# A mixture-of-experts encoder: one half of the activations turned in blocks by VectorE and carried by ScalarE, and the norm weight applied by ScalarE instead of GpSimd

## What is computed

```python
u = rmsnorm(h, norm_ffn_g)                      # row / rms(row) * g, g of 1024 weights
aff = softmax(u @ router_w)                     # per token, over 16 experts
gate, idx = top_k(aff.T, 64)                    # each expert picks 64 of the 512 tokens
xs = u[idx]                                     # 64 rows x 1024; 128 rows for both trunks
hid = silu(xs @ w_gate[e]) * (xs @ w_up[e])     # 128 x 2048
out = (hid @ w_down[e]) * gate
h[idx] += out
```

## Time and profile before

| | |
|---|---|
| median of 3 runs | 1543.75 us |
| the profiled execution's own time | 1543.18 us |
| its span, first to last instruction | 1541.4 us |
| TensorE matmul, busy | 1529.7 us, 99% |
| VectorE, busy | 1309.9 us, 85% |
| ScalarE, busy | 1043.1 us, 68% |
| GpSimd, busy | 225.9 us, 15% |

### The profile page before, as it was taken

The page is one execution under the profiler, slowest core; times in us unless marked ns, Lnnn a source line. Parts: engine busy times, 40 slices in busy tenths (PEclk is TensorE's granted clock), DMA queues, the critical chain, the costliest instruction groups (busy, mean ns, idle before and its releaser), DMA issues.

```text
span 1541.4 us, 22566 instructions
## 1 busy us (share of the span) xinstructions
PE 1529.7 (99%) x8318; PEld 1236.9 (80%) x8318; DVE 1309.9 (85%) x1386; ACT 1043.1 (68%) x985; POOL 225.9 (15%) x140
## 2 busy tenths in 40 slices
PE   9999999999999999999999999999999999999997
PEld 7888878888863888888888888888888888888886
DVE  7684886684865999999999999999999999998987
ACT  6454655353452777777777777777778777777777
POOL 0000010000022222120221303022120312210012
PEclk9999999999999999999999999999999999999999
DMA  9543447333476999999999999999999999999998
GB/s 344 188 144 118 148 146 278 96 124 123 149 255 232 409 419 404 387 414 372 405 389 395 400 377 414 361 421 392 379 405 385 406 382 403 389 385 409 365 395 330
DMA packets 156407, 498.60 MB, mean 323 GB/s; under 512 B 10880, under 2 KB 36608, under 8 KB 156352
## 3 DMA queue, kind: packets, MB, share of 16 engines
q1 hardware_dynamic: 144624, 461.54, 77.1%
q0 software_dynamic: 9280, 31.07, 6.5%
q10 hardware_dynamic: 2448, 5.25, 1.3%
HBM read 473.70 MB, written 20.97 MB: 321 GB/s over the span
## 4 chain that ended last, share of the span: by engine, by line
PE 96%; DMA 1%; DVE 1%; ACT 1%; issue 0%; SPq 0%; POOLq 0%; POOL 0%; DVEq 0%; ACTq 0%
PE ps L1977 81%; PE ps L2025 4%; PE ps L2032 2%; PE ps L2136 2%; PE ps L2076 1%; PE ps L2445 1%; PE ps L2294 1%; PE ps L2082 1%; DMA u_rows<-arena 1%; DMA raw<-w_qkv 0%; PE ps L2582 0%; PE ps L2290 0%; PE ps L2312 0%; DVE arena L1388 0%; SPq L591 0%
## 5 line engine op out<-in xcount | busy, mean ns | idle before, releaser
L1314 DVE TENSOR_TENSOR w_rest<-raw,w_high 128x2048 fp32r<-128x2048 f32 x212 | 506.9, 2402 | 65.8 <-ACT w_high L1191 48.0
L1191 ACT CAST w_high<-raw 128x2048 fp32r<-128x2048 f32 x184 | 352.5, 1916 | 139.5 <-PE ps L1977 139.5
L1977 PE MATMUL ps<-w_high,xt_high 128*128 128x512 f32 x984 | 304.5, 389 | 0.0
L1977 PE MATMUL ps<-w_rest,xt_high 128*128 128x512 f32 x984 | 304.3, 389 | 0.0
L1977 PE MATMUL ps<-w_high,xt_rest 128*128 128x512 f32 x984 | 304.3, 389 | 0.0
L1977 PEld LDWEIGHTS ps<-w_high,xt_high 128*128 128x128 f32 x984 | 184.6, 188 | 39.2 <-issue 0.8
L1314 DVE TENSOR_TENSOR w_rest<-early,w_high 128x2048 fp32r<-128x2048 f32 x90 | 206.7, 2299 | 10.8 <-ACT w_high L1191 10.7
L1977 PEld LDWEIGHTS ps<-w_high,xt_rest 128*128 128x128 f32 x984 | 184.7, 188 | 38.4
L1977 PEld LDWEIGHTS ps<-w_rest,xt_high 128*128 128x128 f32 x984 | 184.7, 188 | 38.2
L1314 DVE TENSOR_TENSOR w_rest<-raw_more,w_high 128x2048 fp32r<-128x2048 f32 x92 | 206.6, 2284 | 6.1 <-ACT w_high L1191 6.1
L1191 ACT CAST w_high<-early 128x2048 fp32r<-128x2048 f32 x90 | 172.3, 1916 | 58.1 <-PE ps L1977 58.1
(11 more groups left out here) (310 smaller groups left out, 2205.5 us busy)
## 6 DMA issues: line engine op xcount, KB each, us to landing
raw<-w_down SPq DMA_DIRECT2D x64, 1024.0 KB, 7.8
raw<-w_gate SPq DMA_DIRECT2D x62, 1024.0 KB, 8.1
raw<-w_up SPq DMA_DIRECT2D x62, 1024.0 KB, 8.0
raw_more<-w_down SPq DMA_DIRECT2D x32, 1024.0 KB, 8.2
early<-w_down SPq DMA_DIRECT2D x32, 1024.0 KB, 8.7
raw_more<-w_gate SPq DMA_DIRECT2D x31, 1024.0 KB, 8.2
raw_more<-w_up SPq DMA_DIRECT2D x31, 1024.0 KB, 8.4
early<-w_gate SPq DMA_DIRECT2D x31, 1024.0 KB, 8.6
```

What stands on the lines that cost most here:

```text
L1191: nc.scalar.copy(w_high[:, i % SLOTS, :], src).then_inc(high_done, 1)
L1314: nc.vector.tensor_tensor(w_rest[:, j, :], src, w_high[:, j, :].bitcast(F32), ALU.subtract).then_inc(rest_done, 1)
L1977: done = nc.tensor.matmul(out, lhs, rhs, start=start and part == 0, stop=stop and part == 2)
```

## The change

Four things change. The first half of the activations (`acts[0]`) is no longer turned by TensorE within the loop: VectorE transposes the 32 x 32 blocks within each group of 32 partitions (`turn_blocks`), ScalarE copies each of the 16 combinations of a group of token rows and a group of feature columns to its group of partitions (`moves`, 32 rows x 256 floats each), casts the outcome (`moved_high`), and VectorE subtracts (`moved_rest`). GpSimd's product with the norm weight is gone; ScalarE applies it on the turned rows, where a feature is a partition, in 8 activations of 128 x 128 with a scale per partition (`weigh_rows`), which write into another tile. The four loads of the spread norm weight become one small load of a column form. Two semaphores are merged at the start of expert 0.

```diff
 def next_rows(e):                       # GpSimd
     gather(e + 1)
-    pool.wait_ge(gathered, 16 + 16 * QUARTERS * (e + 1))
-    tokens = xg.rearrange("p (t n) -> p t n", t=QUARTERS)
-    weights = piece_g.rearrange("p (t n) -> p t n", t=1).broadcast_to([P, QUARTERS, SPAN])
-    nc.gpsimd.tensor_tensor(tokens, tokens, weights, ALU.mult).then_inc(rows_scaled, 1)
...
-    for a in range(QUARTERS):
-        on, of = slice(a * QUARTER, (a + 1) * QUARTER), slice(a * SPAN, (a + 1) * SPAN)
-        pool.dma_start(piece_g[on, :], g_ffn[:, of].broadcast_to([QUARTER, SPAN])).then_inc(grow_in, 16)
+    pool.wait_ge(nmx_done, HEADS * TRUNKS)
+    pool.dma_start(piece_g, g_ffn_pieces).then_inc(grow_in, 16)
...
+def weigh_rows(e):                      # ScalarE
+    if isinstance(e, int) and e == 1:
+        act.wait_ge(grow_in, 16 * 2)
+    act.wait_ge(rows_turned, e)
+    act.wait_ge(xtr_done, e + 1)
+    for k in range(KC):
+        at = slice(k * P, (k + 1) * P)
+        nc.scalar.activation(weighted_rows[:, at], turned_rows[:, at], ACT.Copy, scale=piece_g[:, k:k + 1]).then_inc(rows_scaled, 1)
...
+def moves(f, lo, hi):                   # ScalarE
+    if lo == 0:
+        act.wait_ge(turn_step, TURN_STEPS * f + 1)
+        act.wait_ge(htr_done, 2 * f + 1)
+    for n in range(lo, hi):
+        a, c = n % QUARTERS, n // QUARTERS
+        tokens, columns = slice(a * QUARTER, (a + 1) * QUARTER), slice(c * QUARTER, (c + 1) * QUARTER)
+        nc.scalar.copy(to_chunks[columns, :, tokens], from_blocks[tokens, :, columns]).then_inc(turn_step, 1)
+
+def moved_high(f):
+    act.wait_ge(turn_step, TURN_STEPS * (f + 1))
+    act.wait_ge(pair_used, pairs_before(f) + 28)
+    nc.scalar.copy(ht[0][0][:, :], shuffled).then_inc(hth_done, 1)
...
 act.wait_ge(gate_done, TRUNKS)          # ScalarE, expert 0
+weigh_rows(1)
 rows_high(1)
...
-highs(0, 30, 33)
+highs(0, 30, 31)
+weigh_rows(2)
+highs(0, 31, 33)
 rows_high(2)
...
 with act.Fori(1, E - 2) as f:
     highs(f, 12, 19)
     step_silu(2 * f + 2, pairs_before(f) + 16, 0)
-    highs(f, 19, 28)
+    highs(f, 19, 24)
+    for i in range(24, 28):
+        highs(f, i, i + 1)
+        moves(f, 2 * (i - 24), 2 * (i - 23))
     step_silu(2 * f + 3, pairs_before(f) + 25, 1)
-    highs(f, 28, 31)
+    for i in range(28, 31):
+        highs(f, i, i + 1)
+        moves(f, 2 * (i - 24), 2 * (i - 23))
+        if i == 28:
+            weigh_rows(f + 2)
     rows_high(f + 2)
-    highs(f, 31, 32)
-    hidden_high(2 * f + 2, 0, 2)
-    highs(f, 32, 36)
-    hidden_high(2 * f + 3, 1, 6, pairs_before(f) + 32)
+    highs(f, 31, 33)
+    moves(f, 14, 16)
+    highs(f, 33, 34)
+    moved_high(f)
+    highs(f, 34, 36)
+    hidden_high(f + 4, 1, 6, pairs_before(f) + 32)
     result(f, pairs_before(f) + 32)
...
+def turn_blocks(f):                     # VectorE
+    dve.wait_ge(turn_step, TURN_STEPS * f)
+    dve.wait_ge(hid_done, 2 * f + 3)
+    nc.vector.transpose(blocks, acts[0]).then_inc(turn_step, 1)
...
 turn_rows(f + 2)                        # VectorE, in the loop
-rests(f, 19, 28)
+rests(f, 19, 21)
+turn_blocks(f)
+rests(f, 21, 28)
 step_hidden(2 * f + 3, 1)
 rests(f, 28, 31)
 rows_rest(f + 2)
-rests(f, 31, 32)
-hidden_rest(2 * f + 2, 0, 2)
-rests(f, 32, 36)
+rests(f, 31, 34)
+moved_rest(f)
+rests(f, 34, 36)
 hidden_rest(2 * f + 3, 1)
...
 def all_turns(e):                       # TensorE; e is a register in the loop
     pe.wait_ge(hid_done, 2 * e + 2)
     pe.wait_ge(htr_done, 2 * e)
     if not isinstance(e, int):
         pe.nop(nofuse=True)
-    hidden_t(acts[0], 2)
+    if isinstance(e, int):
+        hidden_t(acts[0], 2)
     hidden_t(acts[1], 6)
```

More of the change, by code:

```diff
@@ L139 @@
 QUARTERS = P // QUARTER
+MOVES = QUARTERS * QUARTERS
+TURN_STEPS = 1 + MOVES
 SPAN = D // QUARTERS
@@ L163, with encoder_kernel @@
 ROW_BANKS = (4, 6)
-def encoder_kernel(nc, x, x_t, g_mix, g_ffn_col, g_ffn, g_fin, w_qkv, bias, w_o, router_w, w_gate, w_up, w_down, identity, y):
+def encoder_kernel(nc, x, x_t, g_mix, g_ffn_col, g_ffn_pieces, g_ffn, g_fin, w_qkv, bias, w_o, router_w, w_gate, w_up, w_down, identity, y):
     h_dram = nc.dram_tensor("h_rows", [TRUNKS * T, D], F32).ap()
@@ L293, in encoder_kernel @@
         spread_rows = lg
-        piece_g = grow[:, 0:SPAN]
+        piece_g = mx[:, :, :].rearrange("p a i -> p (a i)")
+        weighted_rows = h_more[:, 0, :]
         quadrant = var[:, 27:28]
@@ L302, in encoder_kernel @@
         acts = (silu, hid)
+        blocks, shuffled = arena[:, 0, :], arena[:, 1, :]
+        from_blocks = blocks.rearrange("p (m n) -> p m n", n=P)
+        to_chunks = shuffled.rearrange("p (m n) -> p m n", n=P)
         ht = ((ht_high, ht_rest), (odd_high, odd_rest))
@@ L361, in encoder_kernel @@
         scaled = sem("scaled")
+        turn_step = sem("turn_step")
         rows_scaled = sem("rows_scaled")
@@ L406, in encoder_kernel @@
         third_silu_done, third_hid_done = sem("third_silu_done"), sem("third_hid_done")
-        half_silu = sem("half_silu")
         first_xt_done = sem("first_xt_done")
@@ L739, in _ @@
                     nc.gpsimd.tensor_tensor(early_rows, early_rows, grow[0:CAP, :], ALU.mult).then_inc(early_scaled, 1)
-                    pool.wait_ge(early_scaled, 1)
-                    for a in range(QUARTERS):
-                        on, of = slice(a * QUARTER, (a + 1) * QUARTER), slice(a * SPAN, (a + 1) * SPAN)
-                        pool.dma_start(piece_g[on, :], g_ffn[:, of].broadcast_to([QUARTER, SPAN])).then_inc(grow_in, 16)
+                    pool.wait_ge(nmx_done, HEADS * TRUNKS)
+                    pool.dma_start(piece_g, g_ffn_pieces).then_inc(grow_in, 16)
                 for k in full:
@@ L801, in scatter @@
                                         compute_op=ALU.add).then_inc(scattered, 16)
-            pool.wait_ge(grow_in, 16 * (1 + QUARTERS))
             next_rows(0)
@@ L810, in _ @@
             scatter(E - 2)
-            pool.wait_ge(rows_scaled, E - 1)
+            pool.wait_ge(early_scaled, 1)
+            pool.wait_ge(grow_in, 16 * 2)
             load_grow(g_fin)
@@ L815, in _ @@
             pool.indirect_dma_start(last_h, None, h_dram, last_rows).then_inc(last_in, 16)
-            pool.wait_ge(grow_in, 16 * (2 + QUARTERS))
+            pool.wait_ge(grow_in, 16 * 3)
             for t in SCALED_TILES:
@@ L1158, in rows_high, with hidden_high @@
                     return
-                act.wait_ge(rows_turned, e)
-                nc.scalar.copy(xt_high[:, :], turned_rows).then_inc(xth_done, 1)
-            def hidden_high(s, odd, banks=6, used_by_down=None):
-                act.wait_ge(ht_mm, s + 1)
+                act.wait_ge(rows_scaled, KC * e)
+                nc.scalar.copy(xt_high[:, :], weighted_rows).then_inc(xth_done, 1)
+            def weigh_rows(e):
+                if isinstance(e, int) and e == 1:
+                    act.wait_ge(grow_in, 16 * 2)
+                act.wait_ge(rows_turned, e)
+                act.wait_ge(xtr_done, e + 1)
+                for k in range(KC):
+                    at = slice(k * P, (k + 1) * P)
+                    nc.scalar.activation(weighted_rows[:, at], turned_rows[:, at], ACT.Copy, scale=piece_g[:, k:k + 1]).then_inc(rows_scaled, 1)
+            def hidden_high(turns, odd, banks=6, used_by_down=None):
+                act.wait_ge(ht_mm, turns)
                 if used_by_down is not None:
@@ L1215, in _ @@
             act.wait_ge(first_half, 1)
-            nc.scalar.activation(silu[CAP:P, 0:BANK], ps[0:CAP, 0:BANK], ACT.Silu).then_inc(half_silu, 1)
+            nc.scalar.activation(silu[CAP:P, 0:BANK], ps[0:CAP, 0:BANK], ACT.Silu).then_inc(early_silu, 1)
             step_silu(0, GU_PAIRS - 1)
-            hidden_high(0, 0, 0)
+            hidden_high(1, 0, 0)
             highs(0, 8, 11)
@@ L1222, in _ @@
             act.wait_ge(gate_done, TRUNKS)
+            weigh_rows(1)
             rows_high(1)
             highs(0, 11, 14)
-            hidden_high(1, 1)
+            hidden_high(2, 1)
             highs(0, 14, 21)
@@ L1229, in _ @@
             step_silu(3, pairs_before(0) + 27, 1)
-            highs(0, 30, 33)
+            highs(0, 30, 31)
+            weigh_rows(2)
+            highs(0, 31, 33)
             rows_high(2)
             highs(0, 33, 34)
-            hidden_high(2, 0, 2)
+            hidden_high(3, 0, 2)
             highs(0, 34, 36)
-            hidden_high(3, 1, 6, pairs_before(0) + 32)
+            act.sem_inc(turn_step, TURN_STEPS)
+            hidden_high(4, 1, 6, pairs_before(0) + 32)
             result(0, pairs_before(0) + 32)
@@ L1251, in _ @@
             highs(E - 2, 20, 24)
-            hidden_high(2 * E - 2, 0)
+            hidden_high(E + 2, 0)
             highs(E - 1, 0, D_PAIRS)
@@ L1268, in _ @@
             h_square(0)
-            act.wait_ge(ht_mm, 2 * E)
+            act.wait_ge(ht_mm, E + 3)
             nc.scalar.copy(xt_high[:, 0:BANK], bank(6)).then_inc(hth_done, 1)
@@ L1808, in rows_rest @@
                 dve.wait_ge(xth_done, e + 2)
```

(19 more changed lines are left out.)

## The result

The changed kernel takes 1546.37 us, the median of 15 runs (1545.82 to 1548.23), against 1543.63 us (1542.45 to 1544.32, 15 runs) before: a ratio of 1.002, 95% interval 1.0013 to 1.0028. So it is a little slower, by 2.7 us. That is 0.18%, just inside the 0.2% that I had called no change, though the interval reaches past it. The forecast was 1543.8 and its own range 1540.7 to 1547. The profiled execution spans 1544.8 us; before it was 1541.4.

A forecast was written before the change was run, and what follows sets the result against it. TensorE alone was taken to bound the kernel; per turn, 0.49 us saved less waits of 0.23 and 0.26 left 0.0. Profiled 1543.2 plus 0.57 gave 1543.8 us; own range 1540.7 to 1547, with rivals 1537.2 to 1550.

The forecast's parts named there:

- What is saved: TensorE loses 16 of 32 transposes in 13 turns: 0.49 us per turn, 6.4 us in all, the most possible gain.
- The move: ScalarE's copy of 32 x 256 floats: 0.40 us long, costing 0.42 to the next start.
- The hold: On ScalarE, a changed partition group removes the 0.10 us overlap: cast and two moves take 2.78 us, otherwise 2.42.
- The weighing: ScalarE's 128 x 128 activation with a scale per partition: 0.29 us each, eight in 2.33, behind pair 28's cast.
- The Silu: In ScalarE's queue between pairs 27 and 28: 0.92 us to the next start.
- The chain to pair 31: ScalarE's queue from pair 24's cast at 945.10 to pair 31's cast at 968.63, which started at 964.10 before.
- rival B: ScalarE's small or held instructions before pair 31 cost 0.02 to 0.03 us more each: 6.5 us, 1550; chance 0.27.
- The waits: TensorE waits twice per turn: 0.23 us at pair 31 for its subtraction, 0.26 at pair 33 for `moved_rest`.
- The hand-over of 0.15: TensorE resumes 0.05 us after VectorE's subtraction ends, and its first matmul takes 0.33 instead of 0.23: 0.15 in all.
- The total: Per turn, gain 0.49 us and waits 0.49: nothing left, 0.0 us; 1543.8 us, chance 0.42 for within 0.2%.
- A, no hold: ScalarE's moves overlap like other instructions, TensorE never waits, all 6.4 us stay: 1537.4; chance 0.13.
- C, memory: Transfers are the next limit, so the change doesn't matter: 1543.8 as well, within the 0.42 for no change.

The follow-up runs named there:

- early_weigh: Changed kernel with all 8 weighings of a turn behind pair 21's cast instead of pair 28's, moves unchanged: 1536.31 us.
- one_group: Changed kernel with all 16 moves copying within the first group of 32 partitions, into four tiles, turned half not put together: 1536.02 us.
- silu_order: Changed kernel with moves 4 to 7 in the order 5, 6, 7, 4, so the last before the Silu reads the first group: 1544.52 us.
- one_early: Changed kernel with one of the 8 weighings behind pair 21's cast, the other 7 still behind pair 28's: 1542.51 us.

## Why the prediction came out as it did

- **What is saved.** Predicted 0.49 us per turn; early_weigh, which has nothing left but this, has turns of 66.15 against 66.66: 0.51, and 7.0 us in all where I had 6.4. Right, a little small.
- **The move**, predicted 0.40 long and 0.42 apart: 403 ns and 0.43. **The hold**: right, and decisive, as one_group shows. A cast and two moves took 2.79 us on the mean rather than 2.78, 0.08 us in six; pair 24's and the cast of the rows took 0.01 more each.
- **The weighing**: 0.389 long, eight in 2.36 us instead of 2.33.
- **The Silu.** This is the largest term that was wrong, half of what the chain missed: "Silu 0.92: 957.02". It cost 1.05, because the cast behind it is held by the move ahead of it. I had applied the hold to neighbours only. The page of the Trainium skill cited ahead (VectorE: DVE Perf Modes, Two Vector instructions with no wait between them) words the rule by memory, comparing with the last instruction that read or wrote that memory; read so, it gives the Silu's case, and the traces of ScalarE agree in all five places looked at (1.05, 0.93, 0.93, 1.03, 0.92 us). It is worth 1.7 us (silu_order).
- **The chain to pair 31**: predicted 968.63 - 945.10 = 23.53 us, measured 970.63 - 946.84 = 23.79. The 0.26 missed are the 0.08 and 0.02, the 0.03 and the 0.13 above. I had also counted twelve moves ahead of pair 31's cast where the order has 14, two behind each of pairs 24 to 30; the sum had them all, the count of 18 instructions for its steepness and for rival B did not.
- **The waits**: predicted 0.23 and 0.26 at pairs 31 and 33, measured 0.41 and 0.34, at just those places and for those reasons. The first is not 0.26 longer, as the chain is, since TensorE came to pair 31 later by itself: its three pairs behind the transposes took 8.29 us (966.33 to 974.17 + 0.455) and not 3 x 2.73 = 8.19, because 2.73 is a mean and the first two matmuls behind the transposes are slower too. That this error of 0.10 worked against the other was luck. The hand-over of 0.15 was 0.05 (974.87 to 974.92) and 0.11 at the first wait; at the second it was 0.13 (`moved_rest` ends at 979.38 + 1.22) and 0.10, and this is all that the second wait has over its 0.26.
- **The total**: waits of 0.75 less 0.51 saved make 0.24 of the 0.28 us by which the turns grew; where the other 0.04 lies I don't know. 13 x 0.28 are 3.6 us instead of 0; the profiled spans differ by 3.4, the medians by 2.7. The "nothing is left" was the difference of two terms of 0.49 us, and it was off by more than half of one of them: the balance was right, its zero was not.
- **Expert 0** was taken as covered, and TensorE has no wait there that it did not have before.
- **Rivals.** A, no hold, is refuted by the trace; its time of 1537.4 is near what one_group gives without the hold (1536.0). B, the dearer chain, is what happened in direction, but not by its cause: it wanted 0.02 to 0.03 us more on each small instruction, and a cast with two moves was dearer by 0.01 in all; half of what the chain missed is one held cast. C, memory, is refuted.

## What to carry to other kernels

When work moves from the engine that bounds to a helper, what is left of the gain depends on whether the stretch of the helper's queue ahead of its deadline can bear it, not on what the helper's busy time suggests: ScalarE was busy for 59.8 us of a turn at 1546.4 us and for 59.7 at 1536.3. When a helper's work grows, write out its queue up to the next hand-over, look for instructions in it that have long been ready, and put those where the helper idles; here 8 of them, moved by seven pairs, made 10 us. And where a change makes an old wait pointless (pair 9's), the wait keeps costing until it is taken out.

## What was not expected of the hardware

ScalarE starts an instruction 0.10 us before the end of the one ahead, in all traces shown here, only if the groups of 32 partitions read from SBUF and written to SBUF are those of the last reader and the last writer: 0.30 us from copy to copy in one group, 0.43 where either changes. It remembers the group last read in SBUF across an instruction that reads PSUM. Over 16 copies and their neighbours that was the difference between 1536.0 and 1546.4 us. TensorE took 0.10 to 0.11 us more for the first two matmuls behind each interruption shown here, and behind its own transposes (0.73 at 966.33), even where no gap is seen between the records: in one_early, at pair 31, the lines are 0.45 us apart as always, and the first two matmuls still take 0.73 in place of 0.62.
